# RWKV-7 chunk inverse: the transposed inverse and the middle product change partition halves, and X and Y matmuls alternate

## The reference

```python
def step(S, inp):
    r_t, w_t, k_t, v_t, a_t, b_t = inp
    sa = jnp.einsum('bhvk,bhk->bhv', S, a_t)
    S = S * w_t[:, :, None, :] + sa[..., None] * b_t[:, :, None, :] + v_t[..., None] * k_t[:, :, None, :]
    y = jnp.einsum('bhvk,bhk->bhv', S, r_t)
    return S, y
```

## Time and profile before

| what | value |
|---|---|
| median of 3 runs | 1446.81 us (1445.54 to 1447.75) |
| profiled execution, its own time | 1445.13 us |
| its span | 1443.2 us |
| granted TensorE clock, mean | 0.994 of full |
| TensorE busy with matmuls | 1386.0 us, 96% of the span |
| VectorE, ScalarE, GpSimd busy | 859.2, 696.1, 38.2 us |
| chain that ended last, by engine | TensorE 86%, VectorE 7%, ScalarE 4% |

### The profile page before, as it was taken

How to read it: one execution, slowest core, us unless ns; L and a number is a source line. 1 busy time by engine, 2 the same in 40 slices (tenths; PEclk the granted TensorE clock), 3 DMA queues, 4 the chain that set the end, 5 groups by cost and what they waited for, 6 DMA issues and landing times.

```text
span 1443.2 us, 22799 instructions
## 1 busy us (share of the span) xinstructions
PE 1386.0 (96%) x8450; PEld 1143.4 (79%) x8450; DVE 859.2 (60%) x1236; ACT 696.1 (48%) x1104; POOL 38.2 (3%) x41
## 2 busy tenths in 40 slices
PE   6999999999999999999899989999999998999998
PEld 4888877878788788888776788877888887788887
DVE  4545568866644555555966567656555667465554
ACT  5434456665465454444544333225444556454442
POOL 0000000000000000000000000110000010000000
PEclk9999999999999999999899999999999999999999
DMA  8655546555454565554543000304555651255552
GB/s 278 218 175 174 182 132 208 169 166 188 161 175 147 143 218 174 176 194 154 168 148 115 2 2 31 108 29 149 188 189 179 229 167 41 88 179 188 186 189 103
DMA packets 145515, 220.40 MB, mean 153 GB/s; under 512 B 16752, under 2 KB 65150, under 8 KB 145312
## 3 DMA queue, kind: packets, MB, share of 16 engines
q1 hardware_dynamic: 145440, 219.36, 46.3%
HBM read 218.26 MB, written 1.05 MB: 152 GB/s over the span
## 4 chain that ended last, share of the span: by engine, by line
PE 86%; DVE 7%; ACT 4%; issue 1%; DMA 1%; SPq 0%; POOL 0%; ACTq 0%; DVEq 0%
PE acc L288 12%; PE gp L288 12%; PE acc L290 11%; PE acc L289 11%; PE gp L290 11%; PE gp L289 11%; PE tp L905 1%; DMA sb_raw<-in_ffn_w 1%; PE gp L2644 1%; ACT sb_w_hi L261 1%; PE acc L2660 1%; DVE sb_w_lo L277 1%; PE acc L2657 1%; PE acc L2617 1%; ACT sb_xa_hi L452 1%
## 5 line engine op out<-in xcount | busy, mean ns | idle before, releaser
L277 DVE TENSOR_TENSOR sb_w_lo<-sb_raw,sb_w_hi 128x1024 fp32r<-128x1024 f32 (+1 forms) x380 | 452.2, 1215 | 226.1 <-ACT sb_w_hi L261 224.5
L261 ACT ACTIVATE sb_w_hi<-sb_raw 128x1024 fp32r<-128x1024 f32 (+1 forms) x380 | 388.2, 1053 | 221.2 <-PE acc L290 107.6
L288 PE MATMUL gp<-sb_w_hi,sb_xa_hi 128*128 128x512 f32 (+1 forms) x752 | 300.2, 399 | 12.9 <-DVE sb_xa_lo L459 9.9
L290 PE MATMUL gp<-sb_w_lo,sb_xa_hi 128*128 128x512 f32 (+1 forms) x752 | 292.5, 389 | 0.0
L289 PE MATMUL gp<-sb_w_hi,sb_xa_lo 128*128 128x512 f32 (+1 forms) x752 | 292.1, 388 | 0.0
L288 PEld LDWEIGHTS gp<-sb_w_hi,sb_xa_hi 128*128 128x128 f32 x752 | 142.0, 189 | 46.3 <-issue 10.1
L290 PEld LDWEIGHTS gp<-sb_w_lo,sb_xa_hi 128*128 128x128 f32 x752 | 141.8, 189 | 29.9
L289 PEld LDWEIGHTS gp<-sb_w_hi,sb_xa_lo 128*128 128x128 f32 x752 | 142.2, 189 | 27.1 <-issue 0.5
L288 PE MATMUL acc<-sb_w_hi,sb_mid_hi 128*128 128x512 f32 x408 | 159.1, 390 | 0.0
L290 PE MATMUL acc<-sb_w_lo,sb_mid_hi 128*128 128x512 f32 x408 | 158.9, 389 | 0.0
L289 PE MATMUL acc<-sb_w_hi,sb_mid_lo 128*128 128x512 f32 x408 | 158.7, 389 | 0.0
(11 more groups left out here) (406 smaller groups left out, 1772.5 us busy)
## 6 DMA issues: line engine op xcount, KB each, us to landing
sb_raw<-in_ffn_w SPq DMA_DIRECT2D x264, 256.0 KB, 4.4
sb_raw<-in_mlp_w SPq DMA_DIRECT2D x256, 256.0 KB, 2.9
sb_raw<-in_w_in SPq DMA_DIRECT2D x72, 256.0 KB, 3.2
sb_raw<-in_a_w_rkv SPq DMA_DIRECT2D x48, 256.0 KB, 4.5
sb_raw<-in_xattn_w_kv SPq DMA_DIRECT2D x32, 256.0 KB, 3.4
sb_raw<-in_w_out SPq DMA_DIRECT2D x16, 256.0 KB, 2.9
sb_raw<-in_xattn_w_q SPq DMA_DIRECT2D x16, 256.0 KB, 3.0
sb_raw<-in_xattn_w_o SPq DMA_DIRECT2D x16, 256.0 KB, 3.0
```

The lines of the kernel that those rows point to most:

```text
L261: A.e.activation(w_hi[:, s, :, 0:n], raw[:, r, :, 0:n], ACT.Copy).then_inc(hi_done, 1)
L277: V.e.tensor_tensor(w_lo[:, s, :, 0:n], raw[:, r, :, 0:n], w_hi[:, s, :, 0:n].bitcast(F32), ALU.subtract).then_inc(lo_done, 1)
L288: e.matmul(dst, xh, wh, start=start, stop=False)
L290: return e.matmul(dst, xh, wl, start=False, stop=stop)
```

## The change

In the halves of the 128 partitions the transposed inverse Y and the middle product Z change places: steps 0 to 63 of Y and Z now live in partitions 64 to 127, and steps 64 to 127 in partitions 0 to 63. X stays. For this the columns of a (the first of the four turned slots) are written with their two halves exchanged, and the masks' `upper` with them: the first and third matrices of `mt` have their 128 columns rolled by 64. The right-hand side, which comes from those columns, then lies exchanged too, and the solve's three steps change their quadrants.

- `pe_columns` turns slot 7 by halves: per pair two transposes of 64 rows into 64 columns, one from each half of the partitions. The first half turn of each pair comes before everything else and counts in a new semaphore `half_turned`; TensorE waits for it before the other half turn of the pair.
- `pe_z` works in the two crossed quadrants. In `pe_xy` the X matmuls work in the crossed quadrants and the Y matmuls in the straight ones, and they are issued in turn: for each head two of X, then two of Y. X's semaphore is counted up by its last matmul, ahead of the last two of Y. At the last level there is Y alone.
- `pe_a_mat` reads the exchanged columns; its quadrants stay. `dve_first` copies the first Y from one half to the other. `dve_carry` works in the first half.

```diff
-    put("upper", np.stack([strict, full, strict, full], 1).astype(np.float32))
+    turned = np.roll(strict, HALF, 1)
+    put("upper", np.stack([turned, full, turned, full], 1).astype(np.float32))
...
-            def halves(self):
-                return [(m, slice(c * HALF, (c + 1) * HALF)) for m in range(4) for c in range(2)]
+            def crossed(self):
+                first, second = slice(0, HALF), slice(HALF, P)
+                return (first, second), (second, first)
...
+                def half_turn(j, at, there):
+                    return T.e.transpose(self.stream_banks(s)[2 + j][:, there], self.pair_rows(7, t, g, j)[at, :], ident[at, at])
+
                 for j in range(2):
-                    bank = self.stream_banks(s)[2 + j]
-                    for n, slot in enumerate((7, 4, 2, 5)):
-                        mm = T.e.transpose(bank[:, n * P:(n + 1) * P], self.pair_rows(slot, t, g, j), ident)
-                    mm.then_inc(*T.one(self.turned))
+                    half_turn(j, *self.crossed()[j]).then_inc(*T.one(self.half_turned))
+                for j in range(2):
+                    for n, slot in enumerate((4, 2, 5), 1):
+                        T.e.transpose(self.stream_banks(s)[2 + j][:, n * P:(n + 1) * P], self.pair_rows(slot, t, g, j), ident)
+                    T.e.wait_ge(self.half_turned, 2 * u + j + 1)
+                    half_turn(j, *self.crossed()[1 - j]).then_inc(*T.one(self.turned))
...
-                for m, at in self.halves():
-                    mm = T.e.matmul(gp[at, s, m * HALF:(m + 1) * HALF], self.mt[s][at, m, 0, at], self.x_inv[s][at, m, :], start=True, stop=True)
+                for m in range(4):
+                    for at, there in self.crossed():
+                        mm = T.e.matmul(gp[there, s, m * HALF:(m + 1) * HALF], self.mt[s][at, m, 0, there], self.x_inv[s][at, m, :], start=True, stop=True)
...
-                if n < LEVELS - 1:
-                    for m, at in self.halves():
-                        mm = T.e.matmul(acc[at, s, 512 + m * HALF:512 + (m + 1) * HALF], self.y_inv[s][at, m, :], self.z_buf[s][at, m, :], start=True, stop=True)
-                    mm.then_inc(*T.one(self.x[s]))
-                for m, at in self.halves():
-                    mm = T.e.matmul(acc[at, s, m * HALF:(m + 1) * HALF], self.z_buf[s][at, m, :], self.y_inv[s][at, m, :], start=True, stop=True)
+                for m in range(4):
+                    at_m = slice(m * HALF, (m + 1) * HALF)
+                    if n < LEVELS - 1:
+                        for at, there in self.crossed():
+                            mm = T.e.matmul(acc[at, s, 512:1024][:, at_m], self.y_inv[s][there, m, :], self.z_buf[s][there, m, :], start=True, stop=True)
+                        if m == 3:
+                            mm.then_inc(*T.one(self.x[s]))
+                    for at, there in self.crossed():
+                        mm = T.e.matmul(acc[there, s, 0:512][:, at_m], self.z_buf[s][there, m, :], self.y_inv[s][there, m, :], start=True, stop=True)
                 mm.then_inc(*T.one(self.inv_y[s]))
...
-                    mm = T.e.matmul(acc[0:HALF, s, m * HD:(m + 1) * HD], self.y_inv[s][0:HALF, m, :], self.rhs_buf[s][0:HALF, m, :], start=True, stop=True)
+                    mm = T.e.matmul(acc[0:HALF, s, m * HD:(m + 1) * HD], self.y_inv[s][HALF:P, m, :], self.rhs_buf[s][HALF:P, m, :], start=True, stop=True)
...
-                    mm = T.e.matmul(acc[HALF:P, s, 512 + m * HD:512 + (m + 1) * HD], self.mt[s][0:HALF, m, 0, HALF:P], self.u_buf[s][0:HALF, m, :], start=True, stop=True)
+                    mm = T.e.matmul(acc[0:HALF, s, 512 + m * HD:512 + (m + 1) * HD], self.mt[s][0:HALF, m, 0, 0:HALF], self.u_buf[s][0:HALF, m, :], start=True, stop=True)
...
-                    mm = T.e.matmul(acc[HALF:P, s, m * HD:(m + 1) * HD], self.y_inv[s][HALF:P, m, :], self.rhs_buf[s][HALF:P, m, :], start=True, stop=True)
+                    mm = T.e.matmul(acc[HALF:P, s, m * HD:(m + 1) * HD], self.y_inv[s][0:HALF, m, :], self.rhs_buf[s][0:HALF, m, :], start=True, stop=True)
...
-                for c in range(2):
-                    at = slice(c * HALF, (c + 1) * HALF)
-                    V.e.copy_predicated(self.y_inv[s][at], levels[at, 0, 0, :].unsqueeze(1).to_broadcast([HALF, 4, HALF]),
-                                        self.mt[s][at, :, 0, at]).then_inc(*V.one(self.first_y))
+                for at, there in self.crossed():
+                    V.e.copy_predicated(self.y_inv[s][there], levels[at, 0, 0, :].unsqueeze(1).to_broadcast([HALF, 4, HALF]),
+                                        self.mt[s][at, :, 0, there]).then_inc(*V.one(self.first_y))
```

More of the change, by code:

```diff
@@ L2080, in __init__ @@
                 self.rhs, self.rhs_done, self.u, self.u_done = sem(n + "rhs"), sem(n + "rhs_done"), sem(n + "u"), sem(n + "u_done")
-                self.carry, self.carry_done = sem(n + "carry"), sem(n + "carry_done")
+                self.carry, self.carry_done, self.half_turned = sem(n + "carry"), sem(n + "carry_done"), sem(n + "half_turned")
                 self.y, self.y_done, self.state, self.state_done = sem(n + "y"), sem(n + "y_done"), sem(n + "state"), sem(n + "state_done")
@@ L2627, in pe_a_mat @@
                 for j in range(2):
-                    for c in range(2):
+                    for at, there in self.crossed():
                         for e in range(2):
-                            part, at = slice(e * HD, (e + 1) * HD), slice(c * HALF, (c + 1) * HALF)
-                            mm = T.e.matmul(acc[at, s, e * 512 + j * HALF:e * 512 + (j + 1) * HALF], fm[part, j, 0, at], fm[part, j, 2, at],
+                            part = slice(e * HD, (e + 1) * HD)
+                            mm = T.e.matmul(acc[at, s, e * 512 + j * HALF:e * 512 + (j + 1) * HALF], fm[part, j, 0, there], fm[part, j, 2, at],
                                             start=True, stop=True)
@@ L2907, in dve_carry @@
                 V.e.wait_ge(self.carry, u + 1)
-                r = self.rhs_buf[s][HALF:P].rearrange("p m d -> p (m d)")
-                V.e.tensor_tensor(r, r, acc[HALF:P, s, 512:768], ALU.add).then_inc(*V.one(self.carry_done))
+                r = self.rhs_buf[s][0:HALF].rearrange("p m d -> p (m d)")
+                V.e.tensor_tensor(r, r, acc[0:HALF, s, 512:768], ALU.add).then_inc(*V.one(self.carry_done))
             def dve_state(self, V, u):
```

## The result

| kernel | median of its runs | profiled execution | its span | mean granted clock there |
|---|---|---|---|---|
| before | 1447.19 us (1445.54 to 1449.49, 12 runs) | 1445.13 us | 1443.2 us | 0.994 |
| changed | 1450.61 us (1447.22 to 1459.58, 12 runs) | 1449.48 us | 1447.5 us | 0.993 |

The ratio is 1.0027, with a 95% interval of 1.0016 to 1.0037: 2.3 to 5.4 us slower. I had forecast 1.0 us faster, with a range up to 1449.8.

A forecast was written before the change was run, and what follows sets the result against it. Each unit was bound by a chain of waits through VectorE, TensorE's queue and, in units 1 to 3, ScalarE. Terms -0.28, +0.6, +0.1, -0.45, -0.5 and -0.47 made -1.0 on the median: 1445.8 us, range 1443.2 to 1449.8.

The forecast's parts named there:

- start: Units 0 and 1: transposes add 2 x 0.33 us, X/Y of unit 0's levels 1 and 2 saves 2 x 0.47: -0.28.
- units 1 and 2: Dearer transposes delay ScalarE's column copies and the copy of u: +0.3 us each, +0.6 together.
- unit 3: Transposes cost +0.3 us, less 0.2 gained by Y's earlier end at level 0: +0.1.
- units 4 to 6: Level 2 gains from Y's earlier end, cut off by the copy of u: -0.15 us each, -0.45 in all.
- what follows: Behind the core, TensorE's own queue hands the core's gain on, with no further change.
- The X/Y block: X and Y alternating in four quadrants: 32 records take 0.47 us, X no earlier, Y 0.47 us earlier.
- the first Y copy: VectorE's copies from one half to the other keep their time: 0 taken, 0.8 us in all if slower.
- Rival C: Four quadrants do not overlap in X/Y, which keeps 0.93 us: +5.8 us, 1452.6 us; chance 0.05.
- the price of the transposes: Transposes to the solve's second half: 0.09 us per change of array shape, 0.33 us more per unit, eight times.
- Rival D: TensorE's clock falls to 0.50 in the core, costing 3 to 5 us, some 1450 us; chance 0.03.
- The last iteration: Last unit without transposes: output -0.5 us, level 3 among gate products in TensorE's queue -0.47.
- Rival B: Half transposes dear, 0.18 us more per switch, 0.72 a unit, 5.8 in all: 1451.6 us; chance 0.11.

The follow-up runs named there:

- e2: Changed kernel with slot 7 turned by one full transpose against an identity with columns rolled by 64, instead of two halves; 1444.44 us, ratio 0.9987.
- e1: Kernel before with slot 7 of each pair turned by straight half transposes in all units, X and Y in two quadrants; 1452.97 us, ratio 1.0048.
- e3: Changed kernel with the 16 X matmuls ahead of the 16 Y matmuls, not alternating, in the same quadrants; 1450.78 us, ratio 1.0035.
- e11: Kernel before with straight half transposes in unit 0 alone; 1449.22 us, ratio 1.0014.
- e12: Kernel before with straight half transposes in units 1 to 7 and full ones in unit 0; 1449.72 us, ratio 1.0021.
- e15: Kernel before with straight half transposes in unit 0 alone, repeated for a second profile; 1449.43 us, ratio 1.0016.
- e8: Changed kernel once more, unaltered, for a second profile; 1451.14 us, ratio to the kernel before 1.0034.
- e10: Changed kernel with the rolled identity (e2), its two first Y copies in the other order; 1443.33 us, ratio 0.9977.
- e6: Changed kernel with half transposes grouped: both first halves, the six full ones, both second halves; 1452.15 us, ratio 1.0046.
- e4: Kernel before with X and Y matmuls alternating in pairs in the two quadrants they had; 1449.36 us, ratio 1.0020.
- e5: Changed kernel with the rolled identity (e2), each first Y copy reading its own half, output wrong; 1443.68 us, ratio 0.9981.
- e13: Changed kernel with the rolled identity in unit 0 alone, half transposes in units 1 to 7; 1446.85 us, ratio 1.0005.
- e7: Kernel before with slots 7 and 4 both turned by straight half transposes; 1452.75 us, ratio 1.0047.

## Why the prediction was wrong

Forecast and profiles by stages, from the starts of records, after less before in us:

| stage | forecast | measured |
|---|---|---|
| start: unit 0's transposes to unit 1's pair products | -0.28 | +1.95 |
| units 1 and 2 | +0.6 | +0.94 |
| unit 3 | +0.1 | +0.48 |
| units 4 to 6 | -0.45 | +0.43 |
| last unit, to its output | -0.97 | -0.21 |
| what follows | 0 | +0.8 |

- **The X/Y block** (0.47 us for 32 records, X no earlier, Y 0.47 us earlier) held as a mechanism; its worth was forecast too high. e2 gives its worth without the transposes: 2.6 us in the core, where my sum, with its eight times 0.33 taken out, had 3.6. At the start 0.94 was forecast and 0.90 came (unit 0's transposes to unit 1's pair products, 16.11 for 17.01 us). In the units 4 to 6 0.34 came for 0.48, and the first Y copy's 0.12 us of delay, which I had taken at 0, is about the difference; no run takes it away. Rival C is out: Z, X and Y each write one PSUM bank from two halves at full pace. The Trainium skill, TensorEngine Tiling (Array Packing), Restrictions and Gotchas, says that row tiles cannot access one bank at the same time; the four-quadrant rows of 852.65 to 853.12 speak against it here.
- **The step that failed is the price of the transposes.** I took 0.09 us for a change of shape from the differences between blocks, 0.33 us a unit. It was 0.54 for the block. The steps from halves to a full one and to the solve, put at 0.15, took 0.20, three times; the first step, put at 0.06, nothing, and the three full ones between halves 0.28 for 0.22, twice, since the first of them has its successor 0.17 us behind it and not 0.11. That last part stands in the earlier trace rows already: the first four transposes there, right behind Z, spread by 0.06 us more than the second four. I read the cost of a change up to the first record behind it and left out the step after that. Unit 0 pays more, 0.74 us to its pair products without any lower clock (e1, e3 and e11, 3.16 for 2.42), and I had put it at 0.33 like the others. Behind its block stand full-array products, one change of shape more than before: 1.56 us to the first of them for 0.85.
- **Where the block's price lands.** In the units 1 to 3 I let 0.3 us come out, and it was 0.47 to 0.48; X and Y gave nothing back there (18.13 for 18.15), as forecast for the units 1 and 2; the 0.2 us forecast for unit 3 did not come (18.08 for 18.09). In the units 4 to 6, forecast -0.15 each, -0.34 from X and Y and +0.48 from the transposes make the +0.14 measured. Seven units at some 0.5 make the 3.7 us of e12.
- **Rival D, the clock,** at a chance of 0.03, is the second cause, and in the profile it weighs at least as much as the miss of the transposes: 1.6 us at the start (e15 against e11, the same kernel with and without the stretch, 19.35 for 17.75 us to unit 1's pair products) and 0.8 behind the core. It came, in some executions, with unit 0's half transposes; e8's fall at 936 us stands elsewhere, and no run shows what brought it. The changed kernel's granted clock is 0.9908 in the mean of e8's runs, and 0.9938 for the kernel before beside it.
- **The last iteration** was forecast to gain 0.97 us (output 0.5, level 3 0.47). From the last unit's pair products to its output e2 takes 34.54 and e10 34.26 us for 35.21 before, so 0.7 to 0.95; the changed kernel takes 35.00, with a stall of 0.99 us at 932 in it.
- Rival B was the right kind and half its size: it needed 1.05 us a unit to reach 1451.6, and at 0.54, with the clock's share, the kernel got to 1450.6. Taking terms for independent made the forecast too sure: dear transposes and a lower clock came together.

The ledger in medians: half transposes of the units 1 to 7 +3.7, of unit 0 +3.2, X and Y with the copies -1.9 (e2) to -2.7 (e10), together +4.2 to +5.0, measured +3.4 and +4.5. By the ratios unit 0 is +2.0 to +2.3 and the others +3.0, so the agreement is partly luck. **Best version:** the change with the rolled identity; e10 is 2.7 us below the kernel before (0.9977 [0.9968, 0.9986]).

Left open: why the lower clock comes in some executions and not in others, and why a second stretch follows at 1224 to 1236 us. Open too is the stall named "issue" in the last iteration: 1.53 us in e8, 0.99 in the changed kernel's first profile, 0.76 in e6, 0.74 in e4, 0.65 in e5, 0.64 in e13, 0.3 in e1 and e3, 0.18 in e2, none in the other seven. It comes with full and with half transposes. Weights arriving at the same time don't settle it: e7 and e12 move 378 and 393 GB/s from 929 to 933 us and have no stall, e8 398. What all nine share is that the stall ends 2.2 to 2.6 us behind the start of a 16 KB packet on the queue that the page calls "instruction" (930.56 for the stall that ends at 932.90, 931.80 for e8's at 934.35); the seven others have such packets too. TensorE may have run out of instructions there; that is a guess, since no run moved the packets.

## What to carry to other kernels

A layout that needs data in the other half of the partitions is best had from a permuted identity in a full transpose, not from transposes in pieces: pieces change the array's shape, and four changes more cost 0.54 us a unit here, on a chain that repeats. Before such a change is priced, look at which copy behind the block is waited for (here ScalarE's second one), and price that copy's start rather than the block's length. And spread quadrants together with an order that starts all four at once: the quadrants alone brought about half of the gain, the order alone lost 3 us.

## What the runs showed of the hardware

- A change between 64-row and 128-row transposes makes a step of 0.20 us (0.15 behind two 64-row ones, e7) where steps in one shape take 0.11, and the step behind the first full one is 0.17. A 64-row transpose with 64 columns isn't cheaper than a full one (0.11 in one quadrant).
- Two half transposes in different row halves and banks start at the same moment (860.95 twice).
- TensorE does not start matmuls in the order of the program where they lie in different quadrants: in e3 Y's first start 0.17 us ahead of X's last.
- A transpose against an identity with rolled columns takes as long as one against the plain identity (block 1.02 us in both).
- TensorE fell to half its clock (0.52 to 0.58 over 795.5 to 799 us) behind unit 0's block of half transposes in five of nine profiles, and in none of seven behind the full ones. The first eight pair products behind them then took 2.00 us in the changed kernel instead of 1.14.
- In e8 the clock fell to 0.50 from 936.0 to 949.6 us, 1.65 us behind the end of a stall of 1.53 us; TensorE was busy for all of the 13.6 us, and the last unit took 41.8 us for 35.0.
